# Sample attention: the cache turned in 32x32 blocks by VectorE, the scores as products of 32x32 array tiles

## The reference

```
c_past  = pool_c[pages]            # 4096 x 256, the cached latents of one sequence (32 pages of 128 rows)
kr_past = pool_kr[pages]           # 4096 x 64,  the cached rope keys
s_past  = ql . c_past + qr . kr_past      # 8 heads x 4 tokens = 32 queries, 4096 keys
s_new   = ql . cn + qr . krn              # the 4 new keys, causal
p       = softmax([s_past, s_new] * scale)
o       = p_past . c_past + p_new . cn    # 32 x 256
```

## Time and profile before

| | us |
|---|---|
| median of 3 runs | 1982.15 |
| lowest, highest | 1982.14, 1982.97 |
| the profiled execution: its span | 1986.1 |
| TensorE busy | 1937.0 (98%) |
| VectorE busy | 1384.4 (70%) |
| ScalarE busy | 840.1 (42%) |
| GpSimd busy | 898.6 (45%) |

### The profile page before, as it was taken

One profiled execution on the slowest core, in us unless ns is written; L12 is line 12 of the kernel. 1 busy time (PEld: TensorE's weight loads), 2 busy tenths in 40 slices (PEclk: granted clock), 3 DMA queues, 4 the chain that ended last, 5 costly groups with the idle time before them and its releaser, 6 DMA issues.

```text
span 1986.1 us, 34182 instructions
## 1 busy us (share of the span) xinstructions
PE 1937.0 (98%) x13308; PEld 1783.5 (90%) x13308; DVE 1384.4 (70%) x1800; ACT 840.1 (42%) x1478; POOL 898.6 (45%) x554
## 2 busy tenths in 40 slices
PE   8999999999999999989999999999999999999997
PEld 8999999999898988976667999899999999977776
DVE  2999999986556656645344323798888777747779
ACT  4222222225326776764344111655444454554442
POOL 4965553431110100123330235667888878645542
PEclk9999999999999999999999999999999999999999
DMA  7664442232531000135673433233323222468555
GB/s 231 228 213 169 171 170 97 86 97 99 177 121 35 7 23 17 49 140 190 253 268 107 133 116 100 85 103 113 97 92 96 78 76 86 137 198 304 192 187 178
DMA packets 201566, 264.07 MB, mean 133 GB/s; under 512 B 21661, under 2 KB 141743, under 8 KB 197309
## 3 DMA queue, kind: packets, MB, share of 16 engines
q1 hardware_dynamic: 183632, 189.38, 29.7%
q0 software_dynamic: 8320, 46.27, 6.2%
q10 hardware_dynamic: 9469, 26.36, 3.5%
HBM read 200.25 MB, written 62.57 MB: 132 GB/s over the span
## 4 chain that ended last, share of the span: by engine, by line
PE 63%; issue 16%; DVE 15%; ACT 3%; DMA 2%; ACTq 0%; POOL 0%; DVEq 0%; SPq 0%; another core or an unknown queue 0%
PE ps L3394 14%; PE ps L2738 13%; PE ps L2931 9%; PE ps L3473 6%; PE pst L3394 5%; DVE pst L1989 4%; PE ps L3145 2%; PE pst L3473 2%; PE pst L3010 2%; PE ps L3198 1%; PE pst L3177 1%; DVE hv L2496 1%; PE ps L2999 1%; PE ps L2997 1%; PE pst L3180 1%
## 5 line engine op out<-in xcount | busy, mean ns | idle before, releaser
L1708 POOL TENSOR_TENSOR wlo<-wraw,whi 128x1024 fp32r<-128x1024 f32 x68 | 167.8, 2474 | 354.8 <-ACT whi L972 308.3
L1989 DVE SCALAR_TENSOR_TENSOR pst<-g_ext,wtap,pst 128x512 f32<-128x512 f32 x464 | 306.9, 744 | 0.0
L2738 PE MATMUL ps<-xh,whi 128*128 128x352 f32 x864 | 187.2, 325 | 1.2 <-ACT stat L1068 1.2
L2738 PE MATMUL ps<-xh,wlo 128*128 128x352 f32 x864 | 186.2, 323 | 0.0
L2738 PE MATMUL ps<-xl,whi 128*128 128x352 f32 x864 | 186.0, 323 | 0.0
L2738 PEld LDWEIGHTS ps<-xh,whi 128*128 128x128 f32 x864 | 147.0, 189 | 1.9 <-issue 1.8
L2738 PEld LDWEIGHTS ps<-xh,wlo 128*128 128x128 f32 x864 | 148.3, 188 | 0.0
L2738 PEld LDWEIGHTS ps<-xl,whi 128*128 128x128 f32 x864 | 146.7, 188 | 0.0
L1801 POOL TENSOR_TENSOR wlo<-wraw,whi 128x1024 fp32r<-128x1024 f32 (+1 forms) x12 | 24.2, 2027 | 246.3 <-ACT whi L1152 246.3
L1883 POOL TENSOR_TENSOR wlo<-wraw,whi 128x512 fp32r<-128x512 f32 x60 | 88.3, 1479 | 42.8 <-ACT whi L1494 42.8
L3473 PE MATMUL ps<-whi,x1h 128*128 128x512 f32 x242 | 97.3, 402 | 0.5 <-DVE x1l L2565 0.5
(11 more groups left out here) (521 smaller groups left out, 5731.8 us busy)
## 6 DMA issues: line engine op xcount, KB each, us to landing
inr<-f_d SPq DMA_DIRECT2D x77, 256.0 KB, 3.8
wraw<-in_w_in SPq DMA_DIRECT2D x37, 512.0 KB, 4.0
f_d<-hv SPq DMA_DIRECT2D x22, 528.0 KB, 2.7
tw<-in_w_down SPq DMA_DIRECT2D x22, 512.0 KB, 5.2
tw_d<-tw SPq DMA_DIRECT2D x11, 1024.0 KB
wraw<-in_w_up SPq DMA_DIRECT2D x40, 256.0 KB, 3.6
x1f<-in_w_up SPq DMA_DIRECT2D x36, 256.0 KB, 3.9
x1f<-tw_d SPq DMA_DIRECT2D x24, 256.0 KB, 3.4
```

Of the source, the lines that this page charges most:

```text
L1708: nc.gpsimd.tensor_tensor(wlo[:, n % HL, :], wraw[:, n % RAW, :], whi[:, n % HL, :].bitcast(F32), ALU.subtract).then_inc(lo_done, 1)
L1989: half[x] = link(nc.vector.scalar_tensor_tensor(out=dst, in0=src, scalar=tap(k_), in1=pst[:, x, :], op0=ALU.mult, op1=ALU.add))
L2738: last = nc.tensor.matmul(out[:, c, 0:CH], w[:, k, :], x[:, k, c * CH:(c + 1) * CH], start=(k == 0 and x is hi_x and w is wh), stop=(k == ...
```

## The change

VectorE turns the cache instead of TensorE. One instruction transposes all 32 x 32 blocks of 2048 columns, SBUF to SBUF, with no PSUM between: `turn_rope(b)` once, `turn_latent(b, g)` four times per sequence. After it the partitions of a group of 32 hold 32 components of a block (8 blocks of latents, `LB`, 2 of rope keys, `RB`), the columns the keys that lay on those 32 partitions. So the scores need ten steps of 32 components, and in each step 16 products of 32 x 32 tiles with 256 columns: row group `i` (the group of partitions whose keys they are) and column group `g` (the block of 8 slots). Row group `i` writes bank `1 + i` of `ps6`, column group `g` its partitions `32 g` to `32 g + 31`. The queries must lie on all four partition groups: new products ahead of the stage lay them out there (`query_set`).

```diff
@@ tiles
-        ctb = [at(f"ct{g}", [P, 2, 512], F32, ...) for g in range(8)]
-        kt = [at(f"kt{p}", [P, 2, 2, P], F32, A0 + 16384 + p * 2048) for p in range(4)]
+        QD, LB, RB = 32, KL // 32, DR // 32
+        ctb = [at(f"ct{g}", [P, LB, NTL // 4, QD], F32, (R0 + 8192, R0 + 24576, A0, A0 + 8192)[g]) for g in range(4)]
+        ctr = at("ctr", [P, RB, NTL, QD], F32, A0 + 16384)
+        qrl = [at(f"qrl{x}", [P, NB, LB // 2, HT], F32, (R0 + 20480, R0 + 36864)[x]) for x in range(2)]
+        qrr = at("qrr", [P, NB, RB, HT], F32, X0 + 65536)
+        S4 = ps6[:, 1:5, 0:NTL // 4 * QD]
+        NEW = ps6[:, 0, :]
@@ ScalarE
-            (chunk_a: 8 copies of turned latents, 3 of rope keys per sequence)
             def act_exp(b):
...
+                nc.scalar.activation(by_slot(ex[:, 0:1024]), S4.rearrange("p i (t k) -> p i t k", k=QD), ACT.Exp, ...)
+            def prob_copies(b, turned, new):      # both halves and the new row, VectorE had the second
+            for x in range(LB // 2):              # and RB more
+                nc.scalar.activation(query_set(x), set_in_psum(x), ACT.Copy).then_inc(ql_r, 1)
+            for b in range(NB):
+                act_exp(b)
+                if b == NB - 1:
+                    act.dma_start(wuvp ...)
+                    hi(N3 + 1)
+                prob_copies(b, *((pst, NEW) if b < NB - 1 else (psx[1], pst[:, 1, :])))
+                if b == 0:
+                    hi(N3)
+                if b == NB - 2:
+                    act.wait_ge(spv_done, NB - 1)
+                    values_hi(range(MT), slice(0, EARLY))
@@ GpSimd
             def gather_rope(b, g):
-                    pool.wait_ge(ct_done, 8 * (b - 1) + 2 * g + 1)
+                    pool.wait_ge(ct_done, 5 * (b - 1) + 1)
             def gather_latent(b, g):
-                    pool.wait_ge(spv_done, 2 * (b - 2) + 1 + g // 2)
+                    pool.wait_ge(spv_done, b - 1)
             (order per sequence: 4 rope gathers, 4 latent; lo(N3) at b == 2, lo(N3 + 1) now behind the loop)
@@ VectorE
-            (queries; chunk_v: 8 copies of turned latents, 1 of rope keys; prob_v)
+            def turn_rope(b):
+                if b:
+                    dve.wait_ge(sc_done, b)
+                for g in range(4):
+                    dve.wait_ge(k_in[g], 16 * (b + 1))
+                nc.vector.transpose(ctr[:, :, :, :], kb[:, :, :].rearrange("p t (j k) -> p j t k", k=QD)).then_inc(ct_done, 1)
+            def turn_latent(b, g):
+                dve.wait_ge(c_in_q[b % 2][g], 16 * (b // 2 + 1))
+                nc.vector.transpose(ctb[g][:, :, :, :], cb[b % 2][:, 8 * g:8 * g + 8, :].rearrange("p t (j k) -> p j t k", k=QD)
+                                    ).then_inc(ct_done, 1)
+            dve.wait_ge(ql_p, 3)
+            for x in range(LB // 2, LB):
+                nc.vector.tensor_copy(query_set(x), set_in_psum(x)).then_inc(qc_done, 1)
+            for b in range(NB):
+                turn_rope(b)
+                for g in range(3):
+                    turn_latent(b, g)
+                new_scores(b)
+                if b:
+                    out_copy(b - 1)
+                turn_latent(b, 3)
+                group_max(b)
@@ TensorE
+            for x in range(LB):
+                for half in range(2):
+                    c = x % 2 * 256 + half * P
+                    for i in range(4):
+                        nc.tensor.matmul(ps6[i * QD:(i + 1) * QD, 2 + x // 2, c:c + P], qlr[:, half, x * QD:(x + 1) * QD],
+                                         ident[:, :], start=True, stop=True)
+            pe.wait_ge(qr_t, 3 * H)
+            for x in range(RB):
+                for i in range(4):
+                    last = nc.tensor.matmul(ps6[i * QD:(i + 1) * QD, 0, x * 256:(x + 1) * 256], ident[:, x * QD:(x + 1) * QD],
+                                            qsr[:, :, :].rearrange("p h n -> p (h n)"), start=True, stop=True)
+            last.then_inc(ql_p, 1)
-            (turn: 64 latent and 16 rope transposes per sequence)
+            def scores(b):
+                for step, x in enumerate((*range(LB, LB + RB), *range(LB))):
+                    if step == 0:
+                        pe.wait_ge(ct_done, 5 * b + 1)
+                    if step == RB:
+                        pe.wait_ge(ct_done, 5 * b + 5)
+                    for g in range(4):
+                        for i in range(4):
+                            rows = slice(i * QD, (i + 1) * QD)
+                            if x < LB:
+                                w, keys = qrl[x // (LB // 2)][rows, b, x % (LB // 2), :], ctb[g][rows, x, :, :]
+                            else:
+                                w, keys = qrr[rows, b, x - LB, :], ctr[rows, x - LB, 8 * g:8 * g + 8, :]
+                            last = nc.tensor.matmul(S4[g * HT:(g + 1) * HT, i, :], w, keys.rearrange("p t k -> p (t k)"),
+                                                    start=step == 0, stop=step == LB + RB - 1)
+                last.then_inc(sc_done, 1)
-            (pe_sample, weaving two sequences)
+            for b in range(NB):
+                if b:
+                    prob_turn(b - 1, pst, NEW)
+                    values(b - 1)
+                head(b)
+                scores(b)
```

More of the change, by code:

```diff
@@ L225, in program @@
         ex = at("ex", [P, 2 * 512 + NS], F32, A0 + 45056)
-        qc = [at(f"qc{j}", [P, 4, HT], F32, A0 + 49408 + j * 512) for j in range(2)]
         sn = at("sn", [P, NS], F32, A0 + 50432)
@@ L551, in program @@
         kr_parts = ((0, 64, 0), (64, 32, 32), (96, 32, 0))
-        def place(j, u):
-            return psx[(j + u) % 2]
         def count(names):
@@ L1369, in values_hi @@
                     nc.scalar.activation(vth[:, k, cols], vt[:, k, cols], ACT.Copy).then_inc(vh_done, 1)
-            def act_sample(b, j, first=False, last=False):
-                chunk_a(b, j, 0)
-                chunk_a(b, j, 1)
-                if not first:
-                    act_exp(b - 1)
-                chunk_a(b, j, 2)
-                chunk_a(b, j, 3)
-                if not first:
-                    prob_a(b - 1, place(j, 4))
-                for g in range(4, 8):
-                    chunk_a(b, j, g)
-                    if last and g in (4, 7):
-                        act.wait_ge(spv_done, 2 * (NB - 1))
-                        values_hi(range(g - 4, g) if g == 4 else range(4, MT), slice(0, EARLY))
             act.wait_ge(ql_p, 1)
@@ L1835, in _ @@
                         gather_latent(b, g)
-                for g in range(3):
+                for g in range(4):
                     gather_rope(b, g)
@@ L2305, in _ @@
[L2305 to L2315 removed]
+                nc.vector.reduce_max(nmg[:, b:b + 1], mxc[:, :], axis=AX.X, negate=True).then_inc(mf_done, 1)
@@ L3189, in prob_turn @@
                                         ident[:, :])
-                nc.tensor.transpose(W[0:NS, 288:288 + P], ex[:, 1024:], ident[:, :]).then_inc(spt_done, 1)
-            def values(b, j):
-                pe.wait_ge(spt_a, b + 1)
-                pe.wait_ge(spt_v, b + 1)
-                for t in range(8):
-                    for x in range(4):
-                        last = nc.tensor.matmul(W[x * HT:(x + 1) * HT, 0:KL], px[:, t, x * HT:(x + 1) * HT],
-                                                cb[j][:, 16 * (t // 4) + 4 * x + t % 4, :], start=t == 0,
-                                                stop=t == 7 and x > 0)
-                    if t == 3:
-                        last.then_inc(spv_done, 1)
-                nc.tensor.matmul(W[0:HT, 0:KL], pn[:, :], cnr[:, :], start=False, stop=True).then_inc(spv_done, 1)
@@ L3205, in pe_sample @@
-            def pe_sample(b, j, half, first=False):
-                turn(b, j, 0, first, half)
-                if not first:
-                    scores(b - 1, 1 - j, 1)
-                turn(b, j, 1, first, half)
-                turn(b, j, 2, first, half)
-                turn(b, j, 3, first, half)
-                if not first:
-                    pe.wait_ge(ct_a, A_ALL * b + A_CHUNK[2])
-                    pe.wait_ge(ct_v, V_ALL * b + V_CHUNK[2])
-                    prob_turn(b - 1, place(j, 4))
-                turn(b, j, 4, first, half)
-                if not first:
-                    values(b - 1, 1 - j)
-                scores(b, j, 0, first)
-                turn(b, j, 5, first, half)
-                turn(b, j, 6, first, half)
-                head(b, j, first)
-                turn(b, j, 7, first, half)
@@ L3225, in _, with values @@
-            pe.sem_inc(spt_done, 1)
-            pe_sample(0, 0, 0, first=True)
-            for i in range(0, NB // 2 - 1):
-                pe_sample(2 * i + 1, 1, i)
-                pe_sample(2 * i + 2, 0, i + 1)
-            pe_sample(NB - 1, 1, NB // 2 - 1)
-            scores(NB - 1, 1, 1)
+                nc.tensor.transpose(new[0:NS, P:2 * P], ex[:, 1024:], ident[:, :]).then_inc(spt_done, 1)
+            def values(b):
```

(10 more changed lines are left out.)

206 lines of the change are left out of this document (51 added, 155 removed).

## The result

The changed kernel takes 2006.05 us (median of 4, 2002.35 to 2010.06) against 1982.56 for the one before: ratio 1.0122, 95% interval 1.0102 to 1.0142. The forecast was 1990.5. The time lies inside the range of 1958 to 2008 us that took in rival (a), and 4 us above the forecast's own, 1976 to 2002; the move of +23.5 us is near three times the forecast one.

The account below looks back on a forecast made before the run. TensorE was taken to bound the kernel. First scores at 918.1 plus 7 periods of 21.3 us gave last scores at 1067.2 against 1060.9, +6.3; tail +2; 1982.15 + 8.3 = 1990.5 us, range 1958 to 2008.

Parts of the forecast that it names:

- rival (a): Sample attention: the clock holds, period 17.3 us, last scores at 1037.9, total 1959 us; chance 0.25.
- Nothing waits: Cache transfers: 14.0 us per sample, last gather lands near 27 us, wanted at 21.3 + 13.8, so no wait.
- VectorE's turn: Five block turns per sample on VectorE, 2.2 us each back to back, bounds 1.2 and 4.4.
- rival (d): VectorE's block turn takes 4.4 us: period 28.3, first sample +11, total 2048 us; chance 0.05.
- Score steps: TensorE's scores: 16 records of 256 columns in 0.22 us, latent steps 3.48 us per sample at full clock.
- Rival (c): Score products: row groups don't run side by side, latent steps 13.9 us, period 27.8, total 2042; chance 0.10.
- The clock: TensorE's clock falls twice a period and recovers in the dense pieces: period 21.3 us for 17.3, granted clock 0.6 to 0.85.
- (b): TensorE stays at the low clock through all samples: period 26.5 us, total 2029; chance 0.08.
- The second fall: Clock drop after 2.5 us idle ahead of the latent steps: 3 us low and 1.98 full.
- The start: Query layout and first sample with nothing beside it: 23.7 us pass before the first scores stand, at 918.1.
- The tail: Behind the last scores: same order, but first products and last values start at the low clock, +2 us.
- The DMA share: DMA engines' share over the sample attention: near 0.65.

Follow-up runs that it names:

- 1: Changed kernel with latent gathers bringing one cache row of eight from the third sample on (stale data): 2003.94 us, ratio 1.0089 to the kernel before.
- 4: Changed kernel with a sample's latent gathers also waiting for the scores of the sample before: 2013.56 us, ratio 1.0132 to the kernel before.
- 6: Changed kernel with one latent gather in flight at a time from the third sample on: 2023.56 us, ratio 1.0213 to the kernel before.
- 9: The kernel of 1 run again, one cache row of eight gathered: 1987.88 us, ratio 1.0024 to the kernel before.
- 14: Changed kernel with 128 more TensorE instructions (32 one-column products) ahead of the first sample: 2027.51 us, ratio 1.0191 to the kernel before.
- 15: Changed kernel with the fourth latent turn ahead of the new scores and latent gathers issued after six score steps: 2008.85 us, ratio 1.0104 to the kernel before.
- 17: The kernel of 15 run again, early fourth turn and gathers after six score steps: 2005.14 us, ratio 1.0100 to the kernel before.
- 2: Changed kernel with idle TensorE products after each sample's scores and ahead of the latent steps: 2025.64 us, ratio 1.0203 to the kernel before.
- 3: Changed kernel with VectorE's fourth latent turn ahead of the new tokens' scores and output copy: 2021.01 us, ratio 1.0168 to the kernel before.
- 11: The kernel of 3 run again, fourth latent turn ahead of the new scores: 1992.19 us, ratio 1.0054 to the kernel before.
- 5: The changed kernel again, nothing edited, as a control: 2004.84 us, ratio 1.0130 to the kernel before.
- 16: Changed kernel with the early fourth turn and latent gathers issued after four score steps: 2007.29 us, ratio 1.0097 to the kernel before.
- 13: Changed kernel with one cache row of eight gathered and the fourth turn ahead of the new scores: 2007.61 us, ratio 1.0082 to the kernel before.
- 18: The kernel of 13 run again, one row of eight gathered and early fourth turn: 2004.21 us, ratio 1.0097 to the kernel before.

## Why the prediction was wrong

The step that failed is **"Nothing waits"**, in the part on the transfers. It asked only when the latents land and who wants them, and for that it was right: in the changed kernel VectorE never waited for `cb`. What waited was TensorE, for its own instructions, in the queue behind those latents. The sum shows it: the seven periods without their holes are 20.1 to 21.6 us, mean 20.8, against 21.3 forecast; the seven as they are have 23.7. Holes of 20.7 us are more than the error of 15.5 and most of the loss of 23.5; the periods that were 0.5 shorter than forecast and a tail of nothing for +2 took the rest of the error back. That the time still fell inside the range is luck: its upper end stood on no term for this. Experiments 1, 4, 6 and 9 cut the holes down through the transfers, 14 moved them through the program, 15 and 17 cut them down through the order of the two. The rows of before had it in sight: TensorE's records would near double in number, while the earlier trace rows had the DMA engines at 0.97.

Point by point:
- VectorE's turn: 2.2 forecast, 2.277 measured, 2.310 for the rope keys; rival (d) out. The slope of the plain streams was the right row.
- Score steps: 16 records per 0.22 us was right for every other 16 and is 0.31 in the mean. Latent steps without a hole take 4.93 us from first to last start at the full clock (1052.42 to 1057.35), not 3.48: mis-sized by 1.45 a sample. Rival (c) out. The estimate of 5.3 by the Trainium skill ("TensorE: Matmul & The Clock Gate", Part 3, measured speedup) was the nearer; this trace agrees with it within a tenth. What the pause in each step of 32 records is, no run here shows.
- The clock: it fell and came back within each sample; mean over the stage 0.81, inside the forecast 0.6 to 0.85; rivals (a) and (b) out. The values and the new row, priced at 5.6 us, take 5.1 to 6.5, mean 5.7. But they start 5.6 us behind the start of the maximum in the mean, for 6.5 forecast, and VectorE waits 1.4 us a sample for the new scores (9.6 over seven) and not 2.5, so that the latent steps start 14.8 us behind it and not 16.15. The second fall, forecast ahead of the latent steps, did not come: in the seventh sample the clock is full throughout them (the row below). Priced with that fall at 4.98 us, they take 4.93 without it and at the slower rate. In samples 2, 3, 4 and 6 the clock fell in or just behind the hole instead (0.81 and then 0.50 in the fourth), and the records behind it ran low. That these errors cancel, so that the period without holes is 20.8 for 21.3, is luck.
- The start: from the query transposes (887.90) to the first maximum 25.3 us, forecast 25.5.
- The tail: +2 forecast; TensorE is busy for 21.96 of 23.20 us behind the last scores at a clock of 1.00, as before. Zero.
- The DMA share: 0.65 forecast, 0.50 measured (0.55 over 900 to 1060). The forecast was one sample's share; only samples 2 to 7 have latent gathers beside them, and before it was 0.56 over the stage.
- From the query transposes to the last scores: 191.4 us now, 168.3 before, +23.1 for +23.5 in the medians.

The seventh sample's latent steps (stretch, us, TensorE busy, granted clock, DMA, GB/s):

```profile
1052.40:1057.80 5.40, 5.30 (x256) 1.00 0.98 376
```

## What to carry to other kernels

Count instructions and not only their time. A change that trades few long products for many short ones makes the program itself a stream; where it runs beside a burst of gathers that fills the DMA engines, ask for each block who is ahead of it. An idle stretch ended by "issue" on an engine with nothing to wait for, with the DMA share near 1 and a place that drifts by a fixed count of instructions from one round to the next, was that here; starting the gathers just behind the request for the block cut the holes from 3.0 to 4.5 us down to 0.4 to 1.4 without moving less data. And run the unchanged kernel beside each group of edits: here its absence from the first made three experiments (1 to 3) unreadable in their times.

## Not expected of the hardware

- TensorE's instructions come in blocks of 256: a transfer is 16 KB, 118 of them stand against 29,720 products and weight loads of the whole execution (252 each), and two ends lie 128 score records apart (176 and 304 in the last sample of 11). They are asked for about one block ahead: with one row of eight gathered (9) the next block's transfer starts 0.5 to 1.6 us after the end of the one before is reached, and there was no hole of over 1.6 us; with 4 MB of gathers ahead it starts 3.2 to 4.9 us after it in the changed kernel, and the holes are 3.0 to 4.5 (1.9 to 4.1 in 5, 11 and 14).
- In some sessions and not in others, products of 32 x 32 tiles run slowly, some 20 to 28 records in 4.8 us, from 0.9 us behind the start of GpSimd's first of four latent gather issues until 5.7 us behind it, and then at full rate again: shown in its place by 1 against 15 and 16, and by 4. It is 3.5 us a sample. It comes with little data too (1, 13, 18), and no edit brings it: 9 and 11 are the kernels of 1 and 3 without it. It is not the chip either: two chips had one session with it and one without. Why sessions differ stays open; the kernel before was 1985.1 to 1986.9 us in the sessions with it and 1981.2 to 1982.6 in those without.
- 1 MB gathered alone (6) took 6.2 to 7.4 us from its issue to the next one in the third sample, 5.8 to landing in the median from 940 to 1080 us; in the changed kernel, four in flight together, 9.4 in the median to landing.
